# Scatter of the expert outputs: one f32 product with the gates in the matrix, or three bf16 products with zeros and ones

## The chip, the cores and the metric

The kernel runs on one core of one Trainium2 chip. The metric is the device time of one execution in microseconds (us), the median of several. PE is the matrix engine TensorE, DVE is VectorE, ACT is ScalarE, SP the engine that issues most of the DMAs; PSUM is the memory that PE writes, 8 banks of 512 f32 columns.

## The reference

One decoder layer for 320 tokens (256 of a prompt, 64 samples) of width 1024. A mixer (pooling and gated delta rule) comes first, then a mixture of 32 experts of which every token takes 4, then a gated projection of a second input, then the last norm. The part that the change touches is the sum over experts:

```
gates = softmax(top_vals)
gt  = min(x @ w_gate[e] + b_gate[e], 7);  up = clip(x @ w_up[e] + b_up[e], -7, 7)
hid = (up + 1) * (gt * sigmoid(1.702 * gt))
y   = segment_sum((hid @ w_down[e] + b_down[e]) * gate, token)
```

All weights are f32. The 32 experts' three matrices of 1024 x 1024 are 403 MB, which are read once.

## The kernel before, in words

The tokens lie in three tiles (128, 128, 64 rows) in `x3`, the residual. The experts are taken two at a time, 16 **pairs**; two pairs are a **turn**, so 8 turns: the first is written out, turns 1 to 3 are a loop, then comes a place for experts with more tokens than fit (`overflow_block`, not needed with these inputs), turns 4 to 6 are a loop, and turn 7 is written out with a narrower last pair (`final`). Each expert has 64 slots, so that a pair fills 128 rows.

For a pair, `turn_body` on PE (L1481) does this in order: the **gate product** (PSUM banks 0 and 1), the **scatter** of the pair before (`scatter_before`, L1494), the **up product** (banks 2 and 3), the gather of the next pair's rows (`gather`, L1415: a matrix of zeros and ones times the normed rows h, which lie there as three bf16 parts whose sum is the f32 value), the turned gates of the next pair, the turned hidden rows, and the **down product** (banks 4 and 5). Scatter, gather and turns share banks 6 and 7, which are used alternately; each use waits until the engine that empties the bank has done so (semaphores `drained`, `filled`).

The scatter multiplies the pair's results `ybuf` (128 slots x 1024, f32) by `SgT`, the turned matrix that holds at (slot, token) the gate of that token: three tiles times two column halves, six f32 products with 512 columns. DVE adds each to `x3` (`add_rows`). ACT copies y out of PSUM (L967) and sets `y_act`; PE waits for that in front of the scatter (L1559).

The weights stream through `ring`, 8 slots of 2 MB. SP issues a chunk (`load_chunk`, L462) as soon as PE has used the slot's chunk (`chunk_used`); a pair has 12 chunks. The order on every engine is that of the code; nothing is scheduled elsewhere.

Behind the last pair comes the **tail** (PE L1668 to L1706): the second input is turned (`pT0`, `pT1`), the last scatter (`sc00` to `sc21`, first figure the tile, second the half), its product with `w_ple` (`pp..`), the turned normed rows (`tT..`), and the product with `w_ple_gate` (`pg..`). A table gives each of these names a bank and the number of its use (L419 to L430). DVE adds the six scattered pieces (L2307) and marks each tile (`moe0` to `moe2`); ACT squares and sums a marked tile (L1021), DVE norms it (L2314).

## Time and profile before

| | us |
|---|---|
| median of 3 runs | 1225.84 (1225.1 to 1227.18) |
| profiled execution | 1221.89 |
| its span, first to last instruction | 1219.9 |
| PE busy | 1166.0, 96% of the span |
| DVE busy | 376.6, 31% |
| ACT busy | 194.2, 16% |
| PE, records of scatter products in the loop (L1500) | 180, 87.5 busy |

The page lists busy time by engine, a table of 40 slices of the span (30.5 us each), a chain of waits traced back from the last instruction, and the costliest groups of instructions. Its chain gives PE 77% of the span and DMA 16%. An f32 product appears as two records, a bf16 product as one; a record's length includes the way through the array, so it is longer than the step from one to the next.

### The profile page before, as it was taken

To read this page: it belongs to the slowest core of one execution; us is meant where nothing else is said; L and a number is where in the kernel's file an instruction comes from. 1 tells how busy PE (TensorE), PEld (TensorE's weight loads), DVE (VectorE), ACT (ScalarE), POOL (GpSimd) and SP (SyncE) were. 2 spreads that over 40 slices of the span, in tenths; PEclk is the share of its full clock that TensorE was granted. 3 is DMA by queue.
4 is the path that set the end of the run, shared out by engine and by line. 5 is a ranking of instruction groups with operands and counts; after the bars stand their busy time and mean duration, and the time that the engine had idled before them with its cause. 6 is when DMAs were issued, how large, how long until landed. Compare 5 with 4: busy or idle time off the path is not lost.

```text
span 1219.9 us, 14464 instructions
## 1 busy us (share of the span) xinstructions
PE 1166.0 (96%) x5539; PEld 495.9 (41%) x5539; DVE 376.6 (31%) x725; ACT 194.2 (16%) x353; POOL 37.9 (3%) x112
## 2 busy tenths in 40 slices
PE   7999999999999999999999799999999999999996
PEld 5677884433333333333333233333333333232342
DVE  5745674670312121212213012313030312111233
ACT  3532701320101000101010001011010101010134
POOL 5003000000000000000000000000000000000000
PEclk9999999999999999999999899999999999999998
DMA  9811613699999999999999999999999999999911
GB/s 318 269 70 69 227 39 131 250 426 413 428 429 426 427 429 428 428 429 429 428 428 429 426 427 428 428 428 428 429 429 429 429 428 428 427 428 425 408 46 43
DMA packets 49319, 435.03 MB, mean 357 GB/s; under 512 B 6632, under 2 KB 13685, under 8 KB 23665
## 3 DMA queue, kind: packets, MB, share of 16 engines
q1 hardware_dynamic: 44457, 431.60, 85.3%
q10 hardware_dynamic: 4816, 2.81, 0.8%
q8 instruction: 30, 0.49, 0.2%
q14 instruction: 16, 0.13, 0.0%
HBM read 429.54 MB, written 4.11 MB: 355 GB/s over the span
## 4 chain that ended last, share of the span: by engine, by line
PE 77%; DMA 16%; DVE 3%; issue 2%; ACT 2%; SPq 0%; DVEq 0%; ACTq 0%; PEldq 0%
PE ps L1543 43%; DMA ring<-in_w_gate 12%; PE ps L1143 7%; PE ps L1500 7%; PE ps L1190 4%; PE ps L1066 3%; PE ps L1421 3%; PE ps L1330 2%; PE ps L1314 2%; DMA ring<-in_w_up 2%; PE ps L1520 1%; DMA ring<-in_w_in 1%; PE ps L1695 1%; PE ps L1686 1%; PE ps L1321 1%
## 5 line engine op out<-in xcount | busy, mean ns | idle before, releaser
L1543 PE MATMUL ps<-ring,ht_region 128*64 128x512 f32 (+1 forms) x2176 | 451.9, 598 | 14.5 <-DMA ring<-in_w_gate 8.7
L1543 PEld LDWEIGHTS ps<-ring,ht_region 128*64 128x64 f32 (+1 forms) x2176 | 148.0, 134 | 304.2 <-issue 304.2
L1543 PE MATMUL ps<-ring,q_region 128*64 128x512 f32 (+1 forms) x1088 | 223.5, 594 | 0.3 <-ACT q_region L757 0.3
L2183 DVE TENSOR_TENSOR x_resid<-ps,x_resid 128x512 f32<-128x512 f32 (+1 forms) x90 | 62.0, 688 | 424.1 <-PE ps L1500 422.5
L1543 PEld LDWEIGHTS ps<-ring,q_region 128*64 128x64 f32 (+1 forms) x1088 | 71.6, 134 | 144.1 <-issue 143.2
L1143 PE MATMUL ps<-ht_region,ring 128*128 128x320 f32 x320 | 90.2, 441 | 1.9 <-DMA ring<-in_w_in 1.6
L1500 PE MATMUL ps<-u_region,h_region 128*128 128x512 f32 (+1 forms) x180 | 87.5, 616 | 0.0
L1143 PEld LDWEIGHTS ps<-ht_region,ring 128*128 128x128 f32 x320 | 60.9, 193 | 28.5 <-issue 4.7
L954 ACT ACTIVATE q_region<-q_region 128x1024 f32<-128x1024 f32 x16 | 16.9, 1057 | 338.8 <-DVE q_region L2207 338.8
L2225 DVE TENSOR_SCALAR q_region<-ps 128x1024 f32<-128x1024 f32 x15 | 18.4, 1224 | 164.4 <-PE ps L1543 164.4
L967 ACT ACTIVATE u_region<-ps 128x1024 f32<-128x1024 f32 x16 | 16.4, 1024 | 238.0 <-PE ps L1543 238.0
L951 ACT ACTIVATE ht_region<-ps 128x512 f32<-128x512 f32 x30 | 17.9, 597 | 207.0 <-PE ps L1421 207.0
L1500 PEld LDWEIGHTS ps<-u_region,h_region 128*128 128x128 f32 (+1 forms) x180 | 25.2, 170 | 61.3 <-DVE x_resid L2183 40.5
L2183 DVE TENSOR_TENSOR ht_region<-ps,vecs 128x512 f32<-128x512 f32 x30 | 20.7, 691 | 49.4 <-PE ps L1066 47.7
L1421 PE MATMUL ps<-z_region,u_region 128*128 128x512 bf16 x90 | 34.3, 381 | 0.6 <-DVE ht_region L2082 0.6
L1421 PE MATMUL ps<-hmid,u_region 128*128 128x512 bf16 x90 | 34.1, 379 | 0.0
L1520 PE MATMUL ps<-bias_s,ht_region 96*128 96x512 bf16 x96 | 29.3, 387 | 3.3 <-issue 3.3
L1066 PE MATMUL ps<-ident,q_region 128*128 128x128 f32 (+1 forms) x140 | 22.2, 300 | 7.1 <-ACT ht_region L951 6.4
L1330 PE MATMUL ps<-ring,ht_region 128*128 128x512 f32 x64 | 28.6, 595 | 0.0
L1775 DVE SCALAR_TENSOR_TENSOR h_region<-q_region,vecs,h_region 128x256 f32<-128x256 f32 (+1 forms) x72 | 27.7, 385 | 2.6
L1314 PE MATMUL ps<-ring,ht_region 128*128 128x512 f32 x64 | 27.7, 594 | 0.0
L1066 PE MATMUL ps<-ident,ht_region 128*128 128x128 f32 x128 | 23.0, 309 | 2.8 <-ACT q_region L951 2.1
(430 smaller groups left out, 806.9 us busy)
## 6 DMA issues: line engine op xcount, KB each, us to landing
ring<-in_w_gate SPq DMA_DIRECT2D x64, 2048.0 KB, 23.3
ring<-in_w_up SPq DMA_DIRECT2D x64, 2048.0 KB, 21.1
ring<-in_w_down SPq DMA_DIRECT2D x56, 2048.0 KB, 25.9
ring<-in_w_down SPq DMA_DIRECT2D x16, 1024.0 KB, 17.2
ring<-in_w_in SPq DMA_DIRECT2D x5, 2048.0 KB, 15.0
ring<-in_w_out SPq DMA_DIRECT2D x2, 2048.0 KB, 10.3
ring<-in_w_ple_gate SPq DMA_DIRECT2D x1, 4096.0 KB, 25.5
x_resid<-in_x_prompt SPq DMA_DIRECT2D x4, 512.0 KB, 3.9
```

Of the source, the lines that this page charges most:

```text
L1066: return nc.tensor.transpose(out, in_, ident[0:n, 0:n])
L1143: last = mm(ps[:, 0:T], w[:, k, (c % 4) * P:(c % 4 + 1) * P], hT[:, k, :], start=(k == 0), stop=(k == KT - 1))
L1190: last = mm(ps[0:n, h * m:(h + 1) * m], lhs(h), rhs(h), start=True, stop=True)
L1314: last = mm(ps, hT[:, k, t0:t0 + n], w[:, k, hf * 512:(hf + 1) * 512], start=(k == 0), stop=(k == KT - 1))
L1330: last = mm(ps, hT[:, k, t0:t0 + n], wo[:, k, hf * 512:(hf + 1) * 512], start=(k == 0), stop=(k == KT - 1))
L1421: last = mm(ps, Sselb[:, t, :], part(t)[:, hf * 512:(hf + 1) * 512], start=(t == 0 and i == 0), stop=(t == NT - 1 and i == 2))
L1500: mm(ps[0:n, :], SgT[1 - half][:, t, 0:n], ybuf[:, hf * 512:(hf + 1) * 512], start=True, stop=True).then_inc(sm_, 1)
L1520: mm(PS[:, b0 + hf, :], ind[:, half, :], biases[bias][:, hf * 512:(hf + 1) * 512], start=True, stop=False, skip_group_check=True)
L1543: ins = mm(PS[s0_:s0_ + width, b0 + hf, :], lhs[:, k, s0_:s0_ + width], w[a_][:, kk, hf * 512:(hf + 1) * 512], start=False, stop=(k == KT ...
L1775: ins = v.scalar_tensor_tensor(out=out, in0=col(j), scalar=vec("conv_w", j * QKV_T + c), in1=out, op0=ALU.mult, op1=ALU.add)
L2183: lmark(op(*args), drained[b], done)
L2225: lmark(v.tensor_scalar(ubuf, PS[:, 2:4, :].rearrange("p b f -> p (b f)"), LIMIT, -LIMIT, ALU.min, ALU.max), up_act, pair + 2)
```

## The change

The results are multiplied by their gates before the scatter. ACT, while it copies the turned gates of a pair, sums each row (`accum_out`), which gives the slot's gate, since a slot belongs to one token. Then:

- ACT writes `y_hi`, bf16, of gate x y from PSUM; DVE writes gate x y - `y_hi` to `gbuf`; ACT rounds that to `y_mid`, bf16; DVE writes `gbuf` - `y_mid` to `y_lo`, bf16. The sum of the three is gate x y.
- DVE makes `slots_turned`, bf16, a one where the turned gate is over 0.
- PE scatters with three bf16 products for each of the six pieces.
- `y_act` is now set by DVE, when `y_lo` is there.
- The tail does this in column halves, PE with its own order: high parts of a half for all tiles, middle parts, low parts. The first product with `w_ple` comes between the halves. The pieces have other banks: 6, 7, 2 for the first half and 3, 6, 7 for the second. DVE adds all first halves before the second.

```diff
-        ybuf = U[:, 0:1024]
+        y_hi, y_mid = U[:, 0:512].bitcast(BF16), U[:, 512:1024].bitcast(BF16)
+        y_lo = Z[:, 1536:2048].bitcast(BF16)
+        y_psum = PS[:, 4:6, :].rearrange("p b f -> p (b f)")
...
+        gates_turned = [H[:, 3072 + 384 * b:3072 + 384 * b + T] for b in range(2)]
+        slots_turned = U[:, 1216:1408].bitcast(BF16)[:, 0:T]
...
-        for t in range(NT):
-            for hf in range(2):
-                use(f"sc{t}{hf}", 6 + hf)
-        use("hd0", 0), use("hd1", 1), use("pT0", 0), use("pT1", 1)
+        for n, b in (("sc00", 6), ("sc10", 7), ("sc20", 2), ("sc01", 3), ("sc11", 6), ("sc21", 7)):
+            use(n, b)
+        use("hd0", 0), use("hd1", 1), use("pT0", 0), use("pT1", 1), use("pp00", 0)
...
# ACT, in a pair
-                        aux(8, SgT[1 - half].rearrange("p t s -> p (t s)"), 384)
+                        aux(8, gates_turned[1 - half], T, accum_out=slot_gate[:, 1 - half:2 - half])
...
-                    lstep(a.activation(ybuf, PS[:, 4:6, :].rearrange("p b f -> p (b f)"), ACT.Copy),
-                          y_act, i * 2 + half + 2)
...
+                    lstep(a.activation(y_hi, y_psum, ACT.Copy, scale=slot_gate[:, half:half + 1]), yhi_act, pair + 1)
+                    act.wait_ge(yrest, pair + 1)
+                    lstep(a.activation(y_mid, gbuf, ACT.Copy), ymid_act, pair + 1)
# ACT, tail
+            middle(0)
             copy(pT[:, 0, :], bank("pT0")[:, 0:T], "pT0")
             copy(pT[:, 1, :], bank("pT1")[:, 0:T], "pT1")
+            middle(1)
+            copy(ppb[:, 0, 0:512], bank("pp00"), "pp00")
# PE, scatter_before
-                                mm(ps[0:n, :], SgT[1 - half][:, t, 0:n], ybuf[:, hf * 512:(hf + 1) * 512],
-                                   start=True, stop=True).then_inc(sm_, 1)
+                                for part, y in enumerate(y_parts):
+                                    last_ = mm(ps[0:n, :], slots_turned[:, t0:t0 + n], y[:, hf * 512:(hf + 1) * 512],
+                                               start=(part == 0), stop=(part == 2))
+                                last_.then_inc(sm_, 1)
# PE, tail
+            scatter_half(0)
             is_drained(pe, "pT0"), is_drained(pe, "pT1")
...
+            ple_product(0, 0)
+            scatter_half(1)
+            for t, hf in ((0, 1), (1, 0), (1, 1)):
+                ple_product(t, hf)
# DVE, end of a pair
+                        dve.wait_ge(yhi_act, pair + 1)
+                        lmark(v.scalar_tensor_tensor(out=gbuf, in0=y_psum, scalar=slot_gate[:, half:half + 1], in1=y_hi,
+                                                     op0=ALU.mult, op1=ALU.subtract), yrest, pair + 1)
+                        lstep(v.tensor_scalar(slots_turned, gates_turned[half], 0.0, None, ALU.is_gt))
+                        dve.wait_ge(ymid_act, pair + 1)
+                        lmark(v.tensor_tensor(y_lo, gbuf, y_mid, ALU.subtract), y_act, pair + 2)
```

The order on **DVE at the end of the first pair**, before. The first row is the last product of the hidden rows, the two that follow scale the turned rows of the next pair, and the memset begins the next pair's part, whose first work is to load the experts' numbers (`TENSOR_LOAD`) and build their matrices (`u_region<-iotaf,rank`):

```order
L2229 TENSOR_TENSOR q_region<-q_region 128x1024 [waits sig_act,v_loop]
L2183 TENSOR_TENSOR ht_region<-ps,vecs 128x512 [waits filled7,hid_act]
L2183 TENSOR_TENSOR ht_region<-ps,vecs 128x512 [waits filled6,drained7]
L2196 MEMSET small 128x1 [waits drained6]
L2086 TENSOR_LOAD wrout
L2086 ISA x2
L2086 TENSOR_LOAD wrout
L2086 ISA x2
L2073 ISA
L2073 TENSOR_TENSOR u_region<-iotaf,rank 128x3x64
```

and in the changed kernel, at the same place:

```order
L2276 TENSOR_TENSOR q_region<-q_region 128x1024 [waits sig_act,v_loop]
L2230 TENSOR_TENSOR ht_region<-ps,vecs 128x512 [waits filled7,hid_act]
L2230 TENSOR_TENSOR ht_region<-ps,vecs 128x512 [waits filled6,drained7]
L2280 SCALAR_TENSOR_TENSOR q_region<-ps,small,u_region 128x1024 [waits yhi_act,drained6]
L2282 TENSOR_SCALAR u_region<-h_region 128x320 [waits yrest]
L2284 TENSOR_TENSOR z_region<-q_region,u_region 128x1024 [waits ymid_act,v_loop]
L2243 MEMSET small 128x1 [waits y_act]
L2133 TENSOR_LOAD wrout
L2133 ISA x2
L2133 TENSOR_LOAD wrout
L2133 ISA x2
L2120 ISA
```

Three operations with waits for ACT (`yhi_act`, `ymid_act`) now stand between the scaling of the next pair's rows and the memset, that is, in front of the selection and of the adds.

The order on **PE in the tail**, before, from the last scatter (L1592) to the products with `w_ple` (L1686, two instructions each):

```order
L1592 MATMUL ps<-u_region,h_region 128x512 [waits drained6,y_act]
L1592 MATMUL ps<-u_region,h_region 128x512 [waits drained7]
L1592 MATMUL ps<-u_region,h_region 128x512 [waits drained6]
L1592 MATMUL ps<-u_region,h_region 128x512 [waits drained7]
L1592 MATMUL ps<-u_region,h_region 64x512 [waits drained6]
L1592 MATMUL ps<-u_region,h_region 64x512 [waits drained7]
L1686 MATMUL ps<-ring 128x512 [waits drained7,drained1,drained0]
L1686 MATMUL ps<-ring 128x512
L1686 MATMUL ps<-ring 128x512 [waits drained0]
L1686 MATMUL ps<-ring 128x512
L1686 MATMUL ps<-ring 128x512 [waits drained1]
L1686 MATMUL ps<-ring 128x512
```

and in the changed kernel, from the first product with `w_ple` (L1725) over the second half of the scatter (L1716) to the second of these products:

```order
L1725 MATMUL ps<-ring 128x512 [waits drained0,drained1]
L1725 MATMUL ps<-ring 128x512
L1716 MATMUL ps<-u_region 128x512 [waits drained3,yhi_act]
L1716 MATMUL ps<-u_region 128x512 [waits drained6]
L1716 MATMUL ps<-u_region 64x512 [waits drained7]
L1716 MATMUL ps<-u_region 128x512 [waits ymid_act]
L1716 MATMUL ps<-u_region 128x512
L1716 MATMUL ps<-u_region 64x512
L1716 MATMUL ps<-z_region,u_region 128x512 [waits y_act]
L1716 MATMUL ps<-z_region,u_region 128x512
L1716 MATMUL ps<-z_region,u_region 64x512
L1725 MATMUL ps<-ring 128x512 [waits drained7]
```

The scatter has become nine instructions for a half, the middle and low parts wait for ACT and DVE by themselves, and the second product with `w_ple` waits for bank 7, which the last piece of the scatter (third row with L1716) filled.

## Rows read from the trace of the kernel before

**Rows 1.** The page's table by slices: GB/s in each of 40 slices.

```profile
GB/s 318 269 70 69 227 39 131 250 426 413 428 429 426 427 429 428 428 429 429 428 428 429 426 427 428 428 428 428 429 429 429 429 428 428 427 428 425 408 46 43
```

**Rows 2.** Stages: length, busy PE, PEld, DVE, ACT, POOL, then PEclk, DMA share, GB/s.

```profile
300.00:1140.00 840.00, 813.38 (x3684) 288.26 (x3680) 177.78 (x272) 70.78 (x100) 0.00 (x0) 0.99 1.01 428
1052.00:1055.00 3.00, 3.00 (x11) 1.09 (x9) 0.00 (x0) 0.00 (x0) 0.00 (x0) 0.57 1.01 431
```

**Rows 3.** Timeline (start, length, engine, instruction): PE's bias product, two up products apart.

```profile
308.65 0.60 PE L1520 MATMUL ps<-bias_s,ht_region 96*128 96x512 bf16 x2
...
365.24 0.61 PE L1520 MATMUL ps<-bias_s,ht_region 96*128 96x512 bf16 x2
```

**Rows 4.** Timeline of PE: second half of two gate products, idle time before in brackets.

```profile
992.36 7.09 PE L1543 MATMUL ps<-ring,ht_region 128*64 128x512 f32 x32 [1.91 <-DMA ring<-in_w_gate]
...
1051.10 8.78 PE L1543 MATMUL ps<-ring,ht_region 128*64 128x512 f32 x32 [2.08 <-DMA ring<-in_w_gate]
```

**Rows 5.** Weight chunks (L467) issued from 540 to 600, and from 720 to 760.

```profile
DMA to landing us min/median/max: 20.1/25.9/31.4
...
DMA to landing us min/median/max: 14.3/18.9/23.8
```

**Rows 6.** Timeline: a scatter with its first add, first and last gather product.

```profile
645.47 5.82 PE L1500 MATMUL ps<-u_region,h_region 128*128 128x512 f32 x12
...
646.63 0.69 DVE L2183 TENSOR_TENSOR x_resid<-ps,x_resid 128x512 f32<-128x512 f32 x1 [27.68 <-PE ps L1500]
...
665.64 0.39 PE L1421 MATMUL ps<-z_region,u_region 128*128 128x512 bf16 x1
...
669.33 0.38 PE L1421 MATMUL ps<-h_region,u_region 128*128 128x512 bf16 x1
```

**Rows 7.** Single lines: minimum, median, maximum in ns, first and last start.

```profile
L967 ACT ACTIVATE u_region<-ps x16: 1023/1024/1024, 288.6 to 1155.3; 128x1024 f32<-128x1024 f32 x16
...
L2227 DVE SCALAR_TENSOR_TENSOR q_region<-q_region x15: 1224/1225/1226, 267.5 to 1081.5; 128x1024 f32<-128x1024 f32 x15
...
L980 ACT ACTIVATE hmid<-h_region x3: 1057/1057/1057, 254.2 to 256.7; 128x1024 bf16<-128x1024 f32 x3
...
L895 ACT ACTIVATION_READ_ACCUMULATOR h_region<-x_resid x4: 185/186/188, 194.8 to 225.7; 128x1 f32 x3, 64x1 f32 x1
```

**Rows 8.** Timeline at the middle of the loop: DVE's selection, PE behind the fourth turn.

```profile
677.31 0.86 DVE L2073 TENSOR_TENSOR u_region<-iotaf,rank 128x192 bf16<-128x192 f32 x2 [1.89 <-issue]
...
690.86 1.01 PE L1520 MATMUL ps<-bias_s,ht_region 96*128 96x512 bf16 x2 [3.31 <-issue]
696.51 16.09 PE L1543 MATMUL ps<-ring,ht_region 128*64 128x512 f32 x64 [4.64 <-issue]
```

**Rows 9.** Timeline of PE, last pair: up product's second half, turned hidden rows.

```profile
1129.43 7.07 PE L1543 MATMUL ps<-ring,ht_region 128*32 128x512 f32 x64 [1.20 <-DMA ring<-in_w_up]
...
1138.89 0.72 PE L1066 MATMUL ps<-ident,q_region 128*128 128x128 f32 x4 [0.53 <-issue]
```

**Rows 10.** Timeline of the tail: PE, then ACT, then DVE.

```profile
1144.61 10.51 PE L1543 MATMUL ps<-ring,q_region 128*32 128x512 f32 x96
...
1156.35 5.89 PE L1592 MATMUL ps<-u_region,h_region 128*128 128x512 f32 x12
1163.17 7.10 PE L1686 MATMUL ps<-ring 128*128 128x512 f32 x16 [0.94 <-DVE x_resid L2312]
1170.21 0.39 PE L1692 MATMUL ps<-bias_s,zerob 32*128 32x512 bf16 x1
...
1172.39 2.60 PE L1066 MATMUL ps<-ident,h_region 128*128 128x128 f32 x24
...
1156.33 0.91 ACT L757 ACTIVATE ring<-ps 128x320 f32<-128x320 f32 x2
...
1159.19 0.06 DVE L2313 MEMSET small<- 128x1 f32 x1
...
1165.41 0.74 DVE L2317 TENSOR_SCALAR h_region<-x_resid,small 64x1024 f32<-64x1024 f32 x1
```

More of the change, by code:

```diff
@@ L950, in aux @@
                         act.wait_ge(filled[b], done)
-                        lstep(a.activation(out, PS[:, b, 0:width], ACT.Copy), drained[b], done)
+                        lstep(a.activation(out, PS[:, b, 0:width], ACT.Copy, **total), drained[b], done)
                     act.wait_ge(g_act, i * 2 + half + 2)
@@ L2161, in turn_body @@
                 if True:
-                    VPP = 7
+                    VPP = 8
                     for half in range(2):
@@ L2305, in _ @@
             turn_body(TURNS - 1, last=True)
-            for t, (t0, n) in enumerate(TILES):
-                for hf in range(2):
+            mark(v.tensor_scalar(slots_turned, gates_turned[1], 0.0, None, ALU.is_gt), "slots")
+            halves = [slice(0, 512), slice(512, 1024)]
+            for hf, cs in enumerate(halves):
+                dve.wait_ge(yhi_act, PAIRS + hf)
+                step(v.scalar_tensor_tensor(out=gbuf[:, cs], in0=y_psum[:, cs], scalar=slot_gate[:, 1:2], in1=y_hi[:, cs],
+                                            op0=ALU.mult, op1=ALU.subtract), yrest, PAIRS + hf)
+            for hf, cs in enumerate(halves):
+                dve.wait_ge(ymid_act, PAIRS + hf)
+                step(v.tensor_tensor(y_lo[:, cs], gbuf[:, cs], y_mid[:, cs], ALU.subtract), y_act, PAIRS + 1 + hf)
+            for hf, cs in enumerate(halves):
+                for t, (t0, n) in enumerate(TILES):
                     nm = f"sc{t}{hf}"
                     is_filled(dve, nm)
-                    xs = x3[0:n, t, hf * 512:(hf + 1) * 512]
+                    xs = x3[0:n, t, cs]
                     drain(v.tensor_tensor(xs, bank(nm)[0:n, :], xs, ALU.add), nm)
-                mark(v.memset(small[:, 159:160], 0.0), f"moe{t}")
+                    if hf:
+                        mark(v.memset(small[:, 159:160], 0.0), f"moe{t}")
             for t, (t0, n) in enumerate(TILES):
```

61 lines of the change are left out of this document (44 added, 17 removed).

## The prediction

> **What bounds the kernel now.** I read the page by slices first. In [rows 1] the transfers run at 408 to 429 GB/s in 30 of 40 slices, and a table by stages gives most of that stretch in one row: from 300 to 1140 us the DMA share is 1.01 at 428 GB/s, while TensorE is busy 813 of 840 us [rows 2]. Two resources look full, so the next view has to tell which one sets the pace. One pair of experts brings 12 chunks of 2048 KB, 25.17 MB: at 428 GB/s that is 58.8 us. The timeline of PE shows what a pair costs it when nothing is late: from bias product to bias product 365.24 - 308.65 = 56.6 us [rows 3]. So PE starts with a full ring, gains 2.2 us a pair on the transfers, and after some five pairs has eaten its lead; then it waits for a weight chunk, 1.9 and 2.1 us in the rows at 992 and 1051, which is just 58.8 - 56.6 [rows 4]. Those waits are short, but they are where the pace is set: a shorter pair makes them longer and nothing else.
>
> The other half of the test is whether DMA ever runs dry because PE gives slots back late. A chunk takes 4.9 us by itself, and from issue to landing it takes 20.1 us at the least around 540 to 600 and 14.3 us at the least after the middle of the loop [rows 5]. So at least 9.4 us of other chunks stand ahead of every one: DMA is never short of work, and PE may come up to 9 us later at a slot without moving the last landing.
>
> Behind the last pair's wait for w_up (PE resumes at 1129.43) there is no further wait for DMA [rows 9], so from there to the end the path goes through PE, ACT and DVE, and a change there counts in full.
>
> **The change in the 15 scatters inside the loop.** Now: six f32 products of 512 columns. The trace shows each as two records; the group of 12 lasts 5.82 us, and the adds of DVE, 0.69 us each, stand between products on the same bank [rows 6]. New: 18 bf16 products. The gather's 18 of the same form take 669.33 - 665.64 = 3.69 us for 17 steps, 0.217 us each [rows 6], so three are 0.65 us against 0.88 for one f32 product (eight of them without a wait lie between 1163.17 and 1170.21 [rows 10]). Six adds with two banks: product 0.65, then about 0.3 to the add, 0.69 for it, 0.06 back: 1.7 us for two, 4.9 us for six. Saved 0.9 us per pair. ACT's read of the accumulator for the slot's gate adds 0.19 us [rows 7], less 0.06 for 64 fewer columns, between the gather and the turns, where PE waits for ACT already: +0.1. Net -0.8 us per pair, 12 us over 15 pairs on PE. On the end: nothing, since the wait for the chunk takes it. Were that cover gone it would be -12 us.
>
> **The new chain behind the down product.** ACT 1.02 (high part, from PSUM), DVE 1.23 (rest), ACT 1.06 (middle), DVE 1.23 (low) [rows 7], four hand-overs of about 0.05: y is ready 4.7 us after the product, before 1.1. Who is queued behind it: on DVE the selection for the pair after, which so far ran during the product; it began with 1.89 us of loading the expert's number, then four operations, about 3.8 us in all from the memset [rows 8]. Together 8.5 us. PE asks for y only behind the gate product, 14.4 us after the down product, and DVE has to be ready for the adds at the same moment. 5.9 us of slack, cost 0. The step that makes zeros and ones from the turned gates (320 columns) lies in DVE's wait for ACT.
>
> At the middle of the loop PE does wait for y at once (the end of the fourth turn). There it stands 3.6 us longer, in a stretch where it loses 8 us anyway: 3.31 and 4.64 us of "issue", and 16.1 for a product of 13.95 at a lower clock [rows 8]. Bounds: 0 if the 4.64 us are shorter in return, 5.3 if the stand is followed by another 1.7 us like that at 1051. I take 4; both lie under the 9.4 us above, and four pairs at 3.0 us each win it back before the end. Cost 0.
>
> **The last pair.** Four scatters come before w_up's last wait: 0.5 us saved, which makes that wait 1.7 instead of 1.20. The two behind it save 0.6 us of PE, but the next thing PE needs is DVE's hidden half: it stood 0.53 us for that [rows 9]. 0 again. The down product ends at 1155.1 as now.
>
> **The tail**, in the trace's time. ACT high half 0 from 1155.3 to 1155.9, half 1 to 1156.5; DVE rests to 1156.65 and 1157.4; ACT middle 0 to 1157.3, then the two copies of pT (0.91) to 1158.25, middle 1 to 1158.9; DVE low 0 to 1158.1, low 1 (waits for middle 1) to 1159.65. PE: pT turned till 1156.2, three high products to 1157.0, three middle from 1157.4, three low from 1158.2 to 1158.9, pp00 to 1160.65, then half 1: bank 7 waits for sc10's add, done at 1162.7. DVE's adds stand behind low 1: sc00 1160.4, sc10 1161.1, sc20 1161.9; sc01 to 1163.2, sc11, sc21 to 1164.9 with their memsets. Now the point on which the tail turns: pp01 is in bank 7, which sc21 filled, so PE stands from 1162.7 to 1165.05. Then pp01, pp10, pp11, three times 1.76 (7.04 for four [rows 10]), and pp20 as now 2.2. The transposes of h3 begin at 1172.4 to 1172.6, against 1172.39 now [rows 10]. The norm chain ends later, since all first halves are added before any second: from the first tile's mark, 1163.3, it takes the 6.9 us that lie now between 1159.2 and the last tile's 1166.15 [rows 10], so 1170.2, 2.2 us before it is needed. So PE's matmuls get 2 us shorter (18 x 0.217 = 3.9 against 5.9) and stand 2.2 us longer. **Sum of the tail +0.2 us; sum of all +0.2 us.** Bounds of the tail: -2.2 if bank 7 is free in time, +1 if each of the eight hand-overs costs 0.1 more than now. The profiled execution took 1221.89 (span 1219.9 and 2 around it), the median is 1225.84, 3.95 above; I put that on top: 1226.0.
>
> **Rivals.** (B) PE is the bound and the DMA wait an accident of phase: -12 us, 1214. For it: the chain of waits runs mostly through PE. Against: the waits come back pair after pair at the difference of the two periods, and landings take four chunks' time. 5%.
> (C) The tail gains: bank 7 is free early, as the adds go faster than one in 0.75 us: -1 to -2.2, 1224.3. Against: low 1 hangs behind pT's copies. 10%.
> (D) The slower side: PE's new stand before pp01. Behind the wait of 2.08 us at 1051 the granted clock is 0.57 from 1052 to 1055, 1.2 GHz for most of it, and 32 records take 8.78 instead of 7.09 us, +1.7; behind the wait of 1.91 at 992 the same 32 take 7.09, so the clock stayed at 2.4 GHz [rows 2, 4]. The stand of 2.35 us is past that, and from 1165 PE is the path. Alone it gives +1.9 us, 1227.7, within what counts as no change; with the bound of the hand-overs it is +2.9, 1228.7. It decides from a stand of about 2.1 us and a chain 0.6 us longer than my sum. 15%.
> (E) The clock drops at the scatters themselves, with their short gaps: then 18 products take 3.9 us more, a pair 59.7 us, 0.9 over DMA's 58.8, some 13 us, 1239. For it: gaps stay in each scatter. Against: the scatters now have such gaps at two banks, and the row from 300 to 1140 has a clock of 0.99. 4%. The Trainium skill has this as a rule, in "TensorE: Matmul & The Clock Gate", section "A second HAM failure mode: psum-queue depth-cycling": bf16 products of 512 columns that cycle through banks lose the clock in their small idles. By that rule (E) would be the forecast; no row here bears it out.
>
> **Numbers.** Forecast 66%, 1225 to 1227.7 by itself. What a measurement of this kernel can't tell from no change is 0.2%, 2.45 us. Faster: B and a third of C, 0.08. Slower: D and E, 0.19. Same: 0.73. The range from 1224.0 to 1229.0 takes in the forecast, most of C and D.
>
> **What would show it.** Right: pace of the middle at 58.8 us; more of PE's waits for w_gate, near 2.9 us, several followed by slow products, at the same landing times; down product's end near 1155; a stand of about 2.3 us at pp01 for sc21's add; first transpose of h3 near 1172.5. Wrong: the down product's end moved by over 1 us, a DMA share under 1 after the middle, a wait of PE for y in the loop, or no stand at pp01.

## The result, and the profile after

The changed kernel takes 1226.67 us (median of 22 runs, 1223.11 to 1229.3), the kernel before 1224.74 (22 runs, 1222.63 to 1227.18). The ratio is 1.0018, with an interval of 1.0012 to 1.0024: 1.9 us more between the medians, 2.2 by the ratio. It is a slowdown clear of zero, and inside the 0.2% (2.45 us) that counts as no change. The three runs known at the time of the prediction had a median of 1225.84; these 22 have one 1.1 us lower. The profiled execution after has a span of 1224.6 us.

The loop first. Its table by stages has these columns: start and end, length, busy time and count of PE, PEld, DVE, ACT and POOL, then granted clock, DMA share and GB/s. After:

```profile
300.00:1140.00 840.00, 794.14 (x3747) 285.79 (x3772) 215.71 (x311) 87.10 (x127) 0.00 (x0) 0.99 1.01 428
```

Against [rows 2], PE is busy 19 us less, DVE 38 and ACT 16 us more, and the last two figures have not moved: 1.01 of the DMA engines, 428 GB/s. The work on PE was taken out and the transfers went on as before. The timeline of PE (start, length, line, instruction) gives the pair, from bias product to bias product:

```profile
309.50 0.61 PE L1548 MATMUL ps<-bias_s,ht_region 96*128 96x512 bf16 x2
...
365.20 0.61 PE L1548 MATMUL ps<-bias_s,ht_region 96*128 96x512 bf16 x2
```

55.7 us, 0.9 less than in [rows 3]. What became of the 0.9 stands in the waits of PE for DMA, in the same view further on:

```profile
994.34 7.09 PE L1571 MATMUL ps<-ring,ht_region 128*64 128x512 f32 x32 [2.50 <-DMA ring<-in_w_gate]
...
1053.08 7.09 PE L1571 MATMUL ps<-ring,ht_region 128*64 128x512 f32 x32 [2.62 <-DMA ring<-in_w_gate]
...
1131.40 7.07 PE L1571 MATMUL ps<-ring,ht_region 128*32 128x512 f32 x64 [1.99 <-DMA ring<-in_w_up]
1140.86 0.72 PE L1091 MATMUL ps<-ident,q_region 128*128 128x128 f32 x4 [0.97 <-issue]
```

They stand at the same places as in [rows 4] and are 0.6 and 0.5 us longer, and the up product between them lasts 14.26 us (from 1006.76) instead of 13.95; the pair still comes every 58.74 us (1053.08 - 994.34). The wait before the last pair's up product grew from 1.20 to 1.99, and the one behind it from 0.53 to 0.97 [rows 9]. In the same pair PE now waits 2.53 us for w_gate (until 1111.81), where before it had no such wait. What the scatter gave up went into the next wait.

At the middle of the loop one stand of PE is far larger than I had worked out:

```profile
702.42 1.01 PE L1548 MATMUL ps<-bias_s,ht_region 96*128 96x512 bf16 x2 [13.49 <-issue]
703.37 15.78 PE L1571 MATMUL ps<-ring,ht_region 128*64 128x512 f32 x64
```

13.49 us, where [rows 8] have 3.31 and 4.64. The chunks issued behind it, from 720 to 760 us (L475 now, L467 before), tell whether DMA noticed:

```profile
DMA to landing us min/median/max: 10.5/15.1/20.1
```

The least time to landing has shrunk from 14.3 [rows 5] to 10.5 us; a chunk by itself takes 4.9, so over a chunk's transfer still stood ahead of each of these.

Now the tail, PE first and then DVE:

```profile
1157.01 1.21 PE L1091 MATMUL ps<-ident,ring 128*128 128x128 f32 x6
...
1164.85 0.94 PE L1716 MATMUL ps<-z_region,u_region 128*128 128x512 bf16 x3
1167.79 7.11 PE L1725 MATMUL ps<-ring 128*128 128x512 f32 x12 [2.00 <-DVE x_resid L2374]
...
1177.02 2.61 PE L1091 MATMUL ps<-ident,h_region 128*128 128x128 f32 x24
...
1161.93 2.13 DVE L2374 TENSOR_TENSOR x_resid<-ps,x_resid 128x512 f32<-128x512 f32 x3
...
1165.35 0.69 DVE L2374 TENSOR_TENSOR x_resid<-ps,x_resid 128x512 f32<-128x512 f32 x1 [1.28 <-PE ps L1716]
...
1172.33 0.74 DVE L2380 TENSOR_SCALAR h_region<-x_resid,small 64x1024 f32<-64x1024 f32 x1
```

From the first transpose behind the down product (1157.01) to the transposes of h3 (1177.02) it is 20.0 us. Before, that transpose stood at

```profile
1155.05 1.21 PE L1066 MATMUL ps<-ident,ring 128*128 128x128 f32 x6
```

and h3 began at 1172.39 [rows 10], 17.3 us. The tail is 2.7 us longer, which is the whole slowdown and a little more.

The down product itself ends 2.0 us later than before, at 1157.08. Nearly all of that is there when the experts begin. PE's first bias product, before and after:

```profile
236.75 0.59 PE L1520 MATMUL ps<-bias_s,ht_region 96*128 96x512 bf16 x2
...
238.44 0.59 PE L1548 MATMUL ps<-bias_s,ht_region 96*128 96x512 bf16 x2
```

1.7 us. In the fourteen profiles of this case that start lies anywhere from 236.75 to 241.86, and one of the changed loop, without the wait at the middle, has 236.77; so it is not the change. From there to the first transpose of the tail it is 918.3 us before and 918.6 after. The spans of the two profiles differ by 4.7 us: 1.7 ahead of the experts, 0.3 in the pairs, 2.7 in the tail.

In the tail, the stand of 2.00 us at the product of the turned second input is the one that I had foreseen for bank 7. The 12 records of 512 columns behind it (the three products pp01, pp10, pp11) last 7.11 us; 16 of the same kind last 7.10 in [rows 10], so twelve should last 5.3. The clock says why; a stretch that ends within the stand (1165.79 to 1167.79), and one behind it:

```profile
1160.00:1167.00 7.00, 5.79 (x18) 1.74 (x17) 4.54 (x9) 2.40 (x4) 0.00 (x0) 1.00 0.62 251
1168.00:1171.00 3.00, 3.00 (x4) 1.26 (x5) 1.25 (x4) 2.89 (x6) 0.00 (x0) 0.50 0.00 0
```

The granted clock goes from 1.00 (2.4 GHz) to 0.50 (1.2 GHz) behind the stand, and that is worth 7.11 - 5.42 = 1.7 us, as the runs below show. The rest, 1.0, is the stand less what the bf16 products save.

How these products go was not as I had it either. The second half's nine (L1716) begin at 1163.12, and with another bank behind them, in a run below, the next product begins 2.60 us after the first of them: 0.289 each, not 0.217.

### The profile page after: what moved, and what is told of

Its sections match the earlier page's. It is cut to its first block, busy times and chain, and to the rows that moved or that the text cites. A ratio compares the mean times of both kernels' runs of the same rounds, so it can differ in the third digit from the quotient of the medians.

```text
span 1224.6 us, 14773 instructions
## 1 busy us (share of the span) xinstructions
PE 1148.3 (94%) x5604; PEld 493.9 (40%) x5635; DVE 423.0 (35%) x775; ACT 213.7 (17%) x387; POOL 38.0 (3%) x112
## 4 chain that ended last, share of the span: by engine, by line
PE 73%; DMA 18%; DVE 5%; issue 2%; ACT 2%; SPq 0%; DVEq 0%; ACTq 0%; PEldq 0%
PE ps L1571 41%; DMA ring<-in_w_gate 15%; PE ps L1168 7%; PE ps L1527 4%; PE ps L1215 4%; PE ps L1091 3%; PE ps L1446 3%; DMA ring<-in_w_up 2%; PE ps L1355 2%; PE ps L1339 2%; PE ps L1548 1%; DVE x_resid L2230 1%; PE ps L1725 1%; PE ps L1742 1%; PE ps L1465 1%
## 5 line engine op out<-in xcount | busy, mean ns | idle before, releaser
L1571 PE MATMUL ps<-ring,ht_region 128*64 128x512 f32 (+1 forms) x2176 | 452.7, 597 | 16.8 <-DMA ring<-in_w_gate 14.5
L2280 DVE SCALAR_TENSOR_TENSOR q_region<-ps,small,u_region 128x1024 f32<-128x1024 f32 x15 | 19.3, 1284 | 222.2 <-ACT u_region L984 222.2
L984 ACT ACTIVATE u_region<-ps,small 128x1024 bf16<-128x1024 f32 x15 | 16.7, 1114 | 228.1 <-PE ps L1571 228.1
L1527 PE MATMUL ps<-u_region 128*128 128x512 bf16 (+1 forms) x165 | 51.3, 385 | 5.3 <-issue 2.4
L1527 PE MATMUL ps<-z_region,u_region 128*128 128x512 bf16 (+1 forms) x90 | 34.1, 379 | 0.0
L1527 PEld LDWEIGHTS ps<-u_region 128*128 128x128 bf16 (+1 forms) x180 | 12.3, 101 | 47.3 <-DVE x_resid L2230 30.5
L1355 PE MATMUL ps<-ring,ht_region 128*128 128x512 f32 x64 | 28.6, 595 | 0.0
L1446 PE MATMUL ps<-z_region,u_region 128*128 128x512 bf16 x75 | 28.4, 379 | 0.0
(445 smaller groups left out, 918.6 us busy)
```

The costliest lines, as they stand in the source:

```text
L1355: last = mm(ps, hT[:, k, t0:t0 + n], wo[:, k, hf * 512:(hf + 1) * 512], start=(k == 0), stop=(k == KT - 1))
L1446: last = mm(ps, Sselb[:, t, :], part(t)[:, hf * 512:(hf + 1) * 512], start=(t == 0 and i == 0), stop=(t == NT - 1 and i == 2))
L1527: last_ = mm(ps[0:n, :], slots_turned[:, t0:t0 + n], y[:, hf * 512:(hf + 1) * 512], start=(part == 0), stop=(part == 2))
L1571: ins = mm(PS[s0_:s0_ + width, b0 + hf, :], lhs[:, k, s0_:s0_ + width], w[a_][:, kk, hf * 512:(hf + 1) * 512], start=False, stop=(k == KT ...
L2280: lmark(v.scalar_tensor_tensor(out=gbuf, in0=y_psum, scalar=slot_gate[:, half:half + 1], in1=y_hi, op0=ALU.mult, op1=ALU.subtract), yrest, ...
```

## The experiments

The question was, first, whether the loop's edits matter at all; second, what the tail's 2.7 us are made of and what they hang on; third, whether the loop's saving is real and only covered. My theory was the one of the prediction (transfers pace the loop, bank 7 makes PE stand in the tail), with the clock's fall taken in. The rivals: the loop's longer stand at the middle costs the 2 us; the stand in the tail comes from ACT's order rather than from the banks; PE bounds the loop.

### One part alone

The changed loop with the tail of before: the last pair's results are copied unscaled, and the last scatter is the old one.

```
                     if final:
-                        for hf in range(2):
-                            cs = slice(hf * 512, (hf + 1) * 512)
-                            lstep(a.activation(y_hi[:, cs], y_psum[:, cs], ACT.Copy, scale=...), yhi_act, pair + 1 + hf)
+                        lstep(a.activation(ybuf, y_psum, ACT.Copy), y_act, pair + 2)
...
-            scatter_half(0)
+            pe.wait_ge(y_act, PAIRS + 1)
+            for t, (t0, n) in enumerate(TILES):
+                for hf in range(2):
+                    ps = fill(f"sc{t}{hf}")
+                    mm(ps[0:n, :], gates_turned[1][:, t0:t0 + n], ybuf[:, hf * 512:(hf + 1) * 512], start=True, stop=True)
```

> The loop has the three bf16 products, the tail is that of the kernel before (one f32 copy of y, six f32 products with the gates, banks and order of before). Theory A (the loop is paced by the weight transfers, all of the loss is in the tail): within 0.7 us of before, ratio 1.000; the last w_up wait still ends with the landing near 1130, and from the end of the down product to the first transpose of h3 it takes 17.3 us. Theory B (the loss is made in the loop: y ready later, selection behind it on VectorE, the stand at the middle of the loop 4 to 5 us longer, so that the last landings come later): 2 us slower, all of it before the end of the down product.

And the other way round, the loop of before with the changed tail:

```
-                    lstep(a.activation(y_hi, y_psum, ACT.Copy, scale=slot_gate[:, half:half + 1]), yhi_act, pair + 1)
-                    act.wait_ge(yrest, pair + 1)
-                    lstep(a.activation(y_mid, gbuf, ACT.Copy), ymid_act, pair + 1)
+                    lstep(a.activation(ybuf, y_psum, ACT.Copy), y_act, pair + 2)
...
-                                for part, y in enumerate(y_parts):
-                                    last_ = mm(ps[0:n, :], slots_turned[:, t0:t0 + n], y[:, ...], start=(part == 0), ...)
+                                last_ = mm(ps[0:n, :], gates_turned[1 - half][:, t0:t0 + n], ybuf[:, ...], start=True, ...)
```

DVE's three operations at the end of a pair go with them.

> The loop keeps f32 products with the gates in the matrix, the tail is the changed one. Theory A: slower than before by what the whole change costs, 1 to 2.7 us (1.0 from the chain and the stand at pp01, 1.7 more where the clock falls behind that stand), ratio 1.001 to 1.002; down product to first transpose of h3 18.3 us, or 20 with the clock at 1.2 GHz for a stretch. Theory B: no difference from before, 17.3 us.

Measured, beside 1224.57 for before (35 runs): the loop alone 1224.92 (12 runs), ratio 1.0003, 0.9992 to 1.0015; the tail alone 1227.13 (12 runs), 1.0021, 1.0008 to 1.0033. So the slowdown is the tail's, and the loop's edits are worth nothing that a measurement can tell. The loop-only profile has the long stand at the middle too, 13.45 us, and it doesn't cost anything. Its tail reads as before (17.35 us), and the tail-only profile as after:

```profile
1157.18 1.21 PE L1090 MATMUL ps<-ident,ring 128*128 128x128 f32 x6
...
1167.97 7.11 PE L1723 MATMUL ps<-ring 128*128 128x512 f32 x12 [2.00 <-DVE x_resid L2366]
...
1177.20 2.60 PE L1090 MATMUL ps<-ident,h_region 128*128 128x128 f32 x24
```

### The stand in the tail: other banks, and PE kept busy

Four more of the tail's names (pp01, pp10, pp11, pp20) go to banks 4 to 7 in turn instead of 7, 0, 1, 2, so pp01 gets a bank that was free long before. The names behind them in the table (`tT..`, `pg..`) move on likewise.

```
         parts = [f"{t}{hf}" for t in range(NT) for hf in range(2) if t < 2 or hf == 0]
+        rr[0] = 4
         for n in [f"pp{q}" for q in parts[1:]] + ...:
             nxt(n)
```

> As the changed kernel, but pp01, pp10, pp11, pp20 go to banks 4 to 7 in place of 7, 0, 1, 2, so that pp01 does not wait for the add of sc21. Theory A (the stand for bank 7 and the clock behind it are the loss): no stand at pp01; down product to first transpose of h3 16.2 us in place of 20.0, so 1 us faster than before and 3 us faster than the changed kernel, unless the norm chain comes last (it ends 16.1 us after the down product, so it is close). Theory C (the loss is the longer chain of ACT and DVE itself, by way of the norms, and PE only stands because nothing is ready): PE stands as long at the transposes of h3, time as the changed kernel.

Or the stand is left where it is and PE is given nine bf16 products into the unused bank 4 to do meanwhile:

```
             scatter_half(1)
+            for _ in range(9):
+                mm(PS[:, 4, :], slots_turned[:, 0:P], y_lo[:, 0:512], start=True, stop=True)
             for t, hf in ((0, 1), (1, 0), (1, 1)):
```

> As the changed kernel, with nine extra bf16 products of 512 columns into an unused bank right behind the second half of the scatter, 1.95 us, where PE stands 2.0 us for bank 7. They change nothing of the result. Theory A1 (of the 2.7 us of the tail 1.7 are the clock, which falls because PE stands there): the clock stays at 2.4 GHz at pp01 to pp11 (12 records in 5.4 us, not 7.1), time 1 us over before, and 1 to 1.7 us under the changed kernel. Theory A2 (the clock falls for another reason, as the many small gaps of the two halves): still 7.1 us in the runs that have it, time as the changed kernel.

Measured: other banks 1223.45 (11 runs), ratio 0.9990, 0.9980 to 1.0000; filler 1225.97 (12 runs), 1.0011, 1.0001 to 1.0021. PE's timeline with other banks has no stand and no slow product:

```profile
1157.18 1.21 PE L1092 MATMUL ps<-ident,ring 128*128 128x128 f32 x6
...
1165.90 5.42 PE L1726 MATMUL ps<-ring 128*128 128x512 f32 x12
...
1173.43 2.60 PE L1092 MATMUL ps<-ident,h_region 128*128 128x128 f32 x24
```

16.25 us from first to last, 3.8 less than the changed kernel and 1.1 less than before. With the filler, PE and the clock behind the place:

```profile
1156.57 1.21 PE L1091 MATMUL ps<-ident,ring 128*128 128x128 f32 x6
...
1165.29 2.12 PE L1734 MATMUL ps<-z_region,u_region 128*128 128x512 bf16 x9
1167.36 5.42 PE L1725 MATMUL ps<-ring 128*128 128x512 f32 x12
...
1174.90 2.61 PE L1091 MATMUL ps<-ident,h_region 128*128 128x128 f32 x24
```

```profile
1168.00:1171.00 3.00, 3.00 (x9) 1.33 (x8) 1.68 (x4) 2.89 (x6) 0.00 (x0) 1.00 0.00 0
```

The products start at the same moment after the down product as without filler (10.79 us against 10.78), and yet they take 5.42 us at a clock of 1.00. So in the profiles the tail's lengthening falls into two parts: 18.3 - 17.3 = 1.0 us from the stand, net of what the bf16 products save, and 20.0 - 18.3 = 1.7 from the clock that falls behind it. The medians of the whole kernel, 1223.45, 1225.97 and 1226.67, have the order of 16.25, 18.3 and 20.0. The first two are 2.5 apart where the tails say 2.1. The last two, by their ratios to before, are 0.9 apart, give or take some 1.4; that bears out neither 1.7 nor nothing. The clock need not fall in every execution (one profile further down has the stand and keeps it), so its 1.7 us is shown for the profiled executions, and its share of the median is not.

### The stand in the tail: ACT's order

I had argued that DVE's adds come late because the low part of half 1 hangs behind ACT's two copies of pT. Here ACT makes both middle parts first.

```
             middle(0)
+            middle(1)
             copy(pT[:, 0, :], bank("pT0")[:, 0:T], "pT0")
             copy(pT[:, 1, :], bank("pT1")[:, 0:T], "pT1")
-            middle(1)
```

> As the changed kernel, but in the tail ACT rounds the second half's middle part before it copies pT, 0.9 us of copies, so that VectorE's low 1 and all adds come 0.9 us earlier and the stand at pp01 is 1.1 us instead of 2.0. Theory A: 0.9 us less of stand and no fall of the clock behind it: 1 to 2.6 us under the changed kernel, about as before. If the chain is not what PE stands for, no difference from the changed kernel.

Measured 1226.64 (12 runs) beside 1224.26 for before (23 runs), ratio 1.0020, 1.0006 to 1.0033. The expectation was missed. DVE and then PE in that kernel:

```profile
1161.08 2.13 DVE L2374 TENSOR_TENSOR x_resid<-ps,x_resid 128x512 f32<-128x512 f32 x3
1165.31 0.69 DVE L2374 TENSOR_TENSOR x_resid<-ps,x_resid 128x512 f32<-128x512 f32 x1 [2.10 <-PE ps L1716]
...
1167.01 0.68 DVE L2374 TENSOR_TENSOR x_resid<-ps,x_resid 64x512 f32<-64x512 f32 x1
```

```profile
1164.81 0.94 PE L1716 MATMUL ps<-z_region,u_region 128*128 128x512 bf16 x3
1167.75 7.08 PE L1725 MATMUL ps<-ring 128*128 128x512 f32 x12 [2.00 <-DVE x_resid L2374]
```

The first half's adds are done sooner, and DVE then waits 2.10 us instead of 1.28 for PE. What holds pp01 is PE's own low product for the first tile, begun at 1164.81, then three adds of 0.69 us one behind the other with a memset after each; the last of them empties bank 7 at 1167.69. No order on ACT changes that. With both edits, ACT's order and the other banks:

> Changed kernel with both edits of the tail: banks 4 to 7 for pp01 to pp20, and middle 1 ahead of the copies of pT. PE has no stand for the adds, and the norm chain comes 0.9 us earlier than with the banks alone. Theory A: PE's own matmuls now set the tail: down product to first transpose of h3 16.2 us or a little less, 1223.3, 1.1 to 1.5 us under before and not clearly different from the banks alone (0 to 0.5 us less).

Measured 1223.91 (11 runs), ratio 0.9991, 0.9979 to 1.0004: no gain over other banks alone, in the tail 16.25 us like there. Its one profile has something else, in the last pair:

```profile
1133.91 8.59 PE L1572 MATMUL ps<-ring,ht_region 128*32 128x512 f32 x64 [2.73 <-DMA ring<-in_w_up]
```

Here PE resumed 2.6 us later than in the profile with ACT's order alone (1131.35), although both began the experts at 238.47, and the product behind the wait took 8.59 instead of 7.07. Behind that wait nothing hides such a loss; this profiled execution, 1226.9 us, is 3 us over the median of its kernel. One place earlier it is hidden: with ACT's order alone the product behind the last wait for w_gate (2.53 us, as in the changed kernel) took 8.77 instead of 7.07, and the wait for w_up that follows was 0.27 us instead of 1.99.

### The stand in the tail: PE's order

The miss with ACT's order pointed at PE's second half. In the loop the three parts of one tile follow each other into one bank; in the tail one part goes through all three tiles, then the next part. Here half 1, whose parts are all ready by then, goes in the loop's order.

```
             ple_product(0, 0)
-            scatter_half(1)
+            pe.wait_ge(yhi_act, PAIRS + 1)
+            pe.wait_ge(ymid_act, PAIRS + 1)
+            pe.wait_ge(y_act, PAIRS + 2)
+            for t, (t0, n) in enumerate(TILES):
+                ps = fill(f"sc{t}1")
+                for part, y in enumerate((y_hi, y_mid, y_lo)):
+                    last = mm(ps[0:n, :], slots_turned[:, t0:t0 + n], y[:, 512:1024], start=(part == 0), stop=(part == 2))
+                last.then_inc(fsem(f"sc{t}1"), 1)
```

> The changed kernel with the second half of the last scatter in the order of the loop: all three parts of a tile, then the next tile, instead of one part for all tiles, then the next part. The banks, the number of products, ACT and DVE stay. All parts are ready when it starts, 6.1 us behind the first transpose. In the changed kernel these nine products take 2.60 us in the tail, 0.289 each, while those of the loop's scatter and of the gather start 0.217 apart. Theory: the order (another bank and other weights at every product) costs the 0.07 each, so the nine take 1.95 us; the first tile's sum is done 0.65 us after the start instead of 2.0, DVE adds it right behind its adds of the first half (till 7.05), the three adds with their memsets end at 9.4 instead of 10.7, pp01 starts at 9.4 instead of 10.78, its stand is 1.35 instead of 2.00, the transposes of h3 begin 1.3 us earlier (18.7 behind the first transpose) if the clock falls as before and 3.0 earlier if the shorter stand keeps it: time 1225.4 or 1223.7. Rival: each product costs 0.289 here whatever the order (the second half's products are slower in the tail for another reason): then the nine still take 2.60 us, pp01 starts at 9.4 all the same, since the adds set it, but the stand is 0.7 us and the clock should hold: 1223.7. So the length of the group tells the two apart.

Measured 1225.16 (11 runs) beside 1225.18 for before (15 runs): 0.9997, 0.9988 to 1.0006. The slowdown is gone. PE's timeline:

```profile
1158.42 1.21 PE L1091 MATMUL ps<-ident,ring 128*128 128x128 f32 x6
...
1164.54 0.59 PE L1738 MATMUL ps<-u_region 128*128 128x512 bf16 x2
1164.97 0.38 PE L1738 MATMUL ps<-z_region,u_region 128*128 128x512 bf16 x1
1165.19 0.59 PE L1738 MATMUL ps<-u_region 128*128 128x512 bf16 x2
1165.62 0.38 PE L1738 MATMUL ps<-z_region,u_region 128*128 128x512 bf16 x1
...
1167.96 5.42 PE L1725 MATMUL ps<-ring 128*128 128x512 f32 x12 [1.20 <-DVE x_resid L2381]
...
1175.49 2.61 PE L1091 MATMUL ps<-ident,h_region 128*128 128x128 f32 x24
```

From 1164.54 to 1165.62 there are five steps, 0.216 each: the order cost the 0.07 per product, and the rival (0.289 whatever the order) is out. One of the five, from 1164.97 to 1165.19, goes to another tile's bank and weights, and is 0.22 too; so a single such change costs nothing here, and a change at every product does. Whether it is the bank or the weights stays open. The first tile's sum is ready sooner, DVE goes straight from the first half's adds to the second's, pp01 begins 9.54 us behind the first transpose instead of 10.78, the stand is 1.20 us (1.35 expected), the products behind it take 5.42 us. The tail is 17.07 us, 2.9 shorter than in the changed kernel: 1.2 from the earlier bank and 1.7 from the clock, as expected of the case in which the clock holds (17.0). By the medians, each against before in its own runs, it is about 2 us (from +1.9 to 0.0), between the gains of 1.3 and 3.0 that I had given.

### Is the loop's saving real?

To uncover PE, a quarter of each weight chunk isn't loaded, in the kernel before and in the changed one alike; their outputs are not the reference's.

```
-            eng.dma_start(slot(c), w[:, r:r + RPP * P, :].rearrange("a (p k) f -> p (a k) f", p=P)).then_inc(s, 16)
+            rows = w[:, r:r + RPP * P, :].rearrange("a (p k) f -> p (a k) f", p=P)
+            eng.dma_start(slot(c)[:, 0:3], rows[:, 0:3]).then_inc(s, 16)
```

> The kernel before, but of each 2048 KB weight chunk that load_chunk brings only three quarters are loaded (the last quarter of the slot keeps old values, so the outputs are not the reference's). A pair needs 44 us of transfer at 428 GB/s against 56.6 us of PE, so PE sets the pace in all of the loop and the matmuls are the same. Theory A (weight transfers pace the loop now): PE loses its 9.9 us of waits for weights and 1.7 us of lower clock behind one of them: 1213. If the loop is already paced by PE: under 2 us gained.

> The changed kernel with the same three quarters of each chunk (outputs not the reference's). Theory A: the 0.9 us a pair that the bf16 scatter saves on PE, 13 us over the loop, now shows, less the 5 us longer stand of PE in the middle of the loop and the 1 to 2.7 us of the tail: 5 to 7 us under the kernel before with the same loads, about 1207. Theory B (the scatter saves nothing on PE, or the later y makes it wait): the two kernels are equal or this one is slower.

Measured: before with fewer loads 1211.31 (4 runs), 0.9880, 0.9855 to 0.9905; the changed kernel with fewer loads 1203.14 (4 runs), 0.9816, 0.9792 to 0.9841. DMA is no longer full; the tables by stages of the two:

```profile
300.00:1100.00 800.00, 782.51 (x3468) 277.23 (x3468) 170.54 (x262) 69.47 (x98) 0.00 (x0) 0.99 0.82 329
```

```profile
300.00:1100.00 800.00, 776.44 (x3632) 275.72 (x3629) 210.21 (x304) 86.00 (x126) 0.00 (x0) 0.99 0.84 333
```

Now the saving shows: 8.2 us between the two. It adds up. Fifteen pairs at 0.89 are 13.4; the stand at the middle is 12.89 against 3.22 + 6.04 us, 3.6 back; the tail gives back 1.0 (here the same 2.00 us stand is followed by 5.42 us of products, so the clock held): 8.8 by the profiles. It also shows how little the transfers cost before: with PE uncovered the kernel of before is only 13 us faster, 1% of its time, though the periods of PE and DMA, 56.6 and 58.8 us, are 4% apart. The full ring at the start and the stand at the middle let the transfers run ahead, so that in sixteen pairs DMA made PE wait six times only, and never between 639 and 933 us.

### The stand at the middle

PE's wait for y, which it makes at the middle for the overflow experts, moves inside the branch that these inputs don't take.

```
-            pe.wait_ge(y_act, 2 * MID + 1)
...
             with pe.If(n_ov > 0):
+                pe.wait_ge(y_act, 2 * MID + 1)
```

> The changed kernel, but PE's wait for y at the middle of the loop stands inside the branch for overflow experts, which is not taken here; so PE goes on to the ninth pair without it. Theory A (PE's stand there, 13.5 us in place of 8, is covered by the weight transfers): time as the changed kernel, within 1 us. Theory B (the longer stand shifts the last landings): 4 us faster than the changed kernel.

Measured 1226.37 (10 runs) beside 1224.83 for before (21 runs): 1.0012, 0.9999 to 1.0024, as the changed kernel. The stand and the waits of PE (us in total, times, longest) are

```profile
693.11 0.59 PE L1548 MATMUL ps<-bias_s,ht_region 96*128 96x512 bf16 x2 [3.89 <-issue]
```

```profile
PE ps L1571 <- DMA ring<-in_w_gate: 17.3, 8, 3.5
```

9.6 us of standing are gone from the middle, and the kernel takes the same time. The waits for w_gate are eight instead of seven and 17.3 us in total instead of 14.5. That is 2.8 us of the 9.6. Three of the products behind such waits are slow now, at 817, 935 and 1052 us, where none of the changed kernel's behind the middle was; the first two:

```profile
817.58 10.00 PE L1571 MATMUL ps<-ring,ht_region 128*64 128x512 f32 x32 [3.45 <-DMA ring<-in_w_gate]
...
935.02 8.78 PE L1571 MATMUL ps<-ring,ht_region 128*64 128x512 f32 x32 [2.62 <-DMA ring<-in_w_gate]
```

The same 32 records take 7.09 at full clock, so 2.9 and 1.7 us went there, and 1.5 at the third (8.63). That makes 8.9 of the 9.6; the rest isn't followed up row by row. The same edit with a quarter of the loads left out:

> The changed kernel with three quarters of each weight chunk (outputs not the reference's) and without PE's wait for y at the middle of the loop. PE sets the pace here, so what the wait costs shows: 4 to 5 us under the same kernel with the wait (1203.1), about 1198.5, if the wait for y is what lengthens the stand; no difference if the stand comes from loading the code or registers behind it.

Measured 1193.11 (4 runs), 0.9748, 0.9733 to 0.9763: 10.0 us under the changed kernel with fewer loads, where I had expected 4 to 5. Its timeline has a stand of 3.43 us for the 12.89:

```profile
682.69 0.59 PE L1549 MATMUL ps<-bias_s,ht_region 96*128 96x512 bf16 x2 [3.43 <-issue]
```

So the wait costs about twice the 5.1 us by which y is late there (down product's end 688.9, y ready at 694.0 in the changed kernel). The changed kernel's stand would add up as 3.9 for the branch, 5.1 for y and 4.6, the size of the second stand in [rows 8]. That this second stand comes with the wait is an inference: the changed kernel without the wait has none, but the wait was not taken out of the kernel before. What the 4.6 us are isn't settled: in the kernel before, no record of any compute engine lies in them.

### The best of both

The loop of before, the changed tail, and the other banks: the tail-only kernel with `rr[0] = 4`.

> f32 scatter in the loop as before, and in the tail the changed order with pp01 to pp20 in banks 4 to 7. If the loop adds nothing on either side, the same as the banks alone with the changed loop: 0.999 of before, 1223.4. If the longer waits for weights that the shorter scatter leaves cost something by a fall of the clock in the last pair (seen once, 8.59 in place of 7.07 us behind a wait of 2.73), this one is up to 0.5 us faster than the banks alone.

Measured 1223.41 (11 runs) beside 1224.83 (21 runs), ratio 0.9988, 0.9979 to 0.9997. It is 1.4 us faster than before, and equal to the changed kernel with other banks. How much of that is the three-part scatter's is not shown. Before, the first product with `w_ple` stood 0.94 us for its bank [rows 10], and a free bank in the old tail might win most of that by itself: the tail would then be about 16.4 us, an estimate from 17.3 - 0.94, beside 16.25 with the three parts. The old tail with other banks was not run. The other banks and PE's order together were not run; with the other banks no stand is left, so by my estimate the order could give only the 0.6 us of nine faster products.

```profile
1157.65 1.21 PE L1091 MATMUL ps<-ident,ring 128*128 128x128 f32 x6
...
1166.37 5.42 PE L1724 MATMUL ps<-ring 128*128 128x512 f32 x12
...
1173.90 2.61 PE L1091 MATMUL ps<-ident,h_region 128*128 128x128 f32 x24
```

## Why the prediction held, point by point

The range held, and what bounds the loop was right; the sum of the tail did not come out. The forecast was +0.2 us, with PE's clock kept; what came was +1.9, by the way of rival (D), to which I had given 15%. The number looks better than that, 1226.67 for 1226.0, because it was put on a base of 1225.84 and later runs of the kernel before gave 1224.74: that is luck, as is that +1.9 still lies inside what counts as no change.

**What bounds the loop.** Right, and shown. The period of the waits stays 58.7 us, the loop alone measures 1.0003, 9.6 us taken from a stand of PE move the median by 0.3, and PE's saving appears only when the loads shrink. Rival B is out.

**The scatters in the loop.** Net -0.8 us a pair was predicted, -0.9 measured. The changed scatter runs from 647.65 to 652.36, 4.7 us where I had 4.9. DVE's slack in front of the adds was put at 5.9 us; the add at 361.19 had been waiting 6.45.

**The middle of the loop.** I took 3.6 us more, with 5.3 as the bound; it is 13.49 us against the 3.31 + 4.64 = 7.95 of before, 5.5 more, and over the bound. Of that, 4.0 is y, ready 5.1 us after the down product instead of 1.1; the other 1.5 stays open. With fewer loads the difference is 3.6 (12.89 against 9.26), the old second stand being 6.04 there and not 4.64; so differences between profiles are about as large as the 1.5. The answer, nothing on the end, was right, since 5.5 lies under the cover of 9.4 us.

**The last pair.** Right in effect: the wait for w_up grew by 0.8 us where I had 0.5, and the wait of 2.53 us for w_gate I had not foreseen there.

**The tail.** Its order was right in each place: a norm chain that is ready ahead of need (its last step ends at 1173.07, 4 us before the transposes), and a stand before pp01, 2.00 us where the sum had 2.35. Two terms were off. The first is "18 x 0.217 = 3.9": the gather's pace of [rows 6], where three parts follow each other on one tile's matrix into one bank, was taken for products that go from tile to tile. They take 0.289 each, 5.2 us for 18. Counted from the first transpose, half 0 was to be done at 3.8 us and was at 4.3, half 1 at 7.6 and was at 8.7; pp01 began at 10.8 instead of 9.95. There is a wait in it too: the sum had DVE go on from the first half's adds to the second's, and DVE waited 1.28 us for PE's first low product. That turns +0.2 into +1.0. The tail with its second half in the loop's order has 17.07 us, so the order of the parts is worth 1.2 us. By the working of its expectation pp01 begins there at the same time with either pace, so what counts is that the first tile's sum is finished sooner, more than the 0.07 us a product. The second is the clock behind the stand, which I had priced at 1.7 us and given 15%: it came, 1.7 us in the profile, and the filler takes it away. So the profile of the changed kernel is rival (D), "with the bound of the hand-overs it is +2.9", with +2.7 measured and another reason for the longer chain. D's condition, a stand of about 2.1 us, was off: 2.00 was enough in four profiles of five. The forecast held because D lies inside the range and, at 1.9 us between the medians, inside what counts as no change.

**A reason that was wrong though its number was near.** I wrote that the adds are late since "low 1 hangs behind pT's copies". Taking the copies out of the way left the stand at 2.00 us; giving PE another order took it to 1.20.

**Rival C** (bank 7 free in time, -1 to -2.2) did not come about by itself; a change of bank brings it: -1.1 us in the tail, -1.1 by the medians (1223.45 beside 1224.57).

**The signs.** Of those for "right", the pace and the stand at pp01 came. PE's waits for w_gate are seven instead of five, but 2.5 to 2.6 us where I had 2.9, and one of the slow products I had expected behind them is there (8.67 us, at 523), not several. The h3 transposes began at 1177.0, not 1172.5. Of those for "wrong", one came by its letter: the down product's end moved by 2.0 us, of which 1.7 lie ahead of the experts, as said above. Such a sign has to be counted from a point inside the same profile.

**Rival E.** The granted clock in the loop is 0.99 before and after. Within one scatter:

```profile
647.00:653.00 6.00, 5.67 (x25) 1.71 (x24) 4.00 (x6) 0.00 (x0) 0.00 (x0) 1.00 0.99 423
```

Eighteen products of 512 columns that alternate between two banks ran at 2.4 GHz here. The Trainium skill's page "TensorE: Matmul & The Clock Gate", section "A second HAM failure mode: psum-queue depth-cycling", reports of another kernel that bf16 products which cycle through PSUM banks lose the clock in their small idles. This kernel's traces don't agree with it: 1.00 in this window, and 0.99 from 300 to 1140 us, where all fifteen scatters lie.

## What to carry to other kernels

Before making an engine's work in a loop cheaper, compare its period with the period of the transfers: here 56.6 against 58.8 us meant that fifteen savings of 0.9 were worth nothing that a measurement could tell, while one bank in the tail was worth some 3 us of the changed kernel. Where a product waits for a bank, look at which add empties it, and at the order in which the sums are finished: the one that is emptied first should be finished first. A stand on TensorE can cost nearly its length once more, by the products that follow it at half the clock: 1.7 us behind one of 2.00 here. When two resources both look full, cut one of them in an experiment to see whether a saving on the other is real.

## What was unexpected in the hardware

- bf16 products of 512 columns begin 0.217 us apart when three follow each other on the same weights and bank, and 0.289 apart when every one goes to another tile's weights and bank than the one before. A single such change between two groups of three cost nothing (0.22).
- The same stand of 2.00 us at the same place was followed by a clock of 0.50 to 0.56 in four profiles (the changed kernel, the tail alone, ACT's order, no wait at the middle) and by 1.00 in the fifth (fewer loads). In the changed kernel's loop waits of 2.50, 2.53 and 2.62 us kept the clock and one of 2.38 at 523 us lost it (8.67 us for a product of 7.09); the wait of 2.53 at the same place lost it with ACT's order. The length of the stand alone doesn't decide it.
- PE's wait at the place between the two loops cost about twice the time by which the awaited result is late: 12.89 us of standing with it, 3.43 without, for a result 5.1 us late.
- ACT's pass over the down product with a gate for each slot, to bf16, took 1.11 us; the plain copy to f32 took 1.02 [rows 7]. What part is the gate's and what the type's isn't shown. DVE's operation of the same size on PSUM took 1.28 us, the one on tiles outside PSUM 1.23.
